# 32 of 256 prompt tokens go from the dense value products to gathered rows, and gate times activation is formed in place late in the score stage

## What is computed

```python
# per token: eid (8 heads x 16 picks), gate = softmax(top_s)
act = gelu(einsum('chkd,cd->chk', u_emb[eid], xc))
out = einsum('chk,chkd->cd', gate * act, v_emb[eid])
x   = x + gate2 * out
```

## Time and profile before

| what | us |
|---|---|
| median of 3 runs | 1236.54 (1234.68 to 1238.4) |
| span of the profiled execution | 1236.2 |
| score stage, about | 428 to 868 |
| value stage, about | 868 to 1228 |
| TensorE busy | 1200.4 |
| VectorE / GpSimd / ScalarE busy | 920.6 / 617.2 / 596.2 |

### The profile page before, as it was taken

One profiled execution on the slowest core, in us unless ns is written; L12 is line 12 of the kernel. 1 busy time (PEld: TensorE's weight loads), 2 busy tenths in 40 slices (PEclk: granted clock), 3 DMA queues, 4 the chain that ended last, 5 costly groups with the idle time before them and its releaser, 6 DMA issues.

```text
span 1236.2 us, 28223 instructions
## 1 busy us (share of the span) xinstructions
PE 1200.4 (97%) x8839; PEld 1114.8 (90%) x8839; DVE 920.6 (74%) x2251; ACT 596.2 (48%) x1021; POOL 617.2 (50%) x313
## 2 busy tenths in 40 slices
PE   5999999989999999999999999999999999999997
PEld 3888888879989999999999999999888888888886
DVE  3899967957647999779999997000667888888865
ACT  2342546666444445445555454444555555555553
POOL 0475665603755577766666666777203444443101
PEclk9999999999999999999999999999999999999999
DMA  9786674424643466665555555667877898888773
GB/s 356 247 294 211 221 254 176 159 69 164 243 149 125 138 216 199 211 193 182 178 187 179 181 184 180 216 208 241 278 240 271 314 341 307 305 300 308 270 238 105
DMA packets 115996, 273.12 MB, mean 221 GB/s; under 512 B 32033, under 2 KB 56321, under 8 KB 115553
## 3 DMA queue, kind: packets, MB, share of 16 engines
q1 hardware_dynamic: 107760, 248.96, 59.5%
q0 software_dynamic: 6448, 19.71, 4.5%
q10 hardware_dynamic: 1728, 3.68, 0.9%
HBM read 249.30 MB, written 23.00 MB: 220 GB/s over the span
## 4 chain that ended last, share of the span: by engine, by line
PE 90%; issue 2%; DVE 2%; DMA 2%; POOL 2%; ACT 1%; SPq 1%; DVEq 0%; POOLq 0%; ACTq 0%
PE ps L2305 19%; PE ps L2247 11%; PE ps L2254 11%; PE ps L2248 11%; PE ps L2308 10%; PE ps L1909 7%; PE ps L1925 7%; PE ps L1919 6%; PE ps L2283 2%; DMA ring<-in_stream 2%; POOL split L683 1%; PE ps L1941 1%; PE ps L2013 1%; PE ps L1863 1%; PE ps L2224 1%
## 5 line engine op out<-in xcount | busy, mean ns | idle before, releaser
L750 POOL TENSOR_TENSOR split<-ring,split 128x1024 fp32r<-128x1024 f32 x128 | 307.4, 2402 | 138.7 <-ACT split L1051 138.7
L1051 ACT ACTIVATE split<-ring 128x1024 fp32r<-128x1024 f32 x256 | 271.6, 1061 | 173.5 <-PE ps L2305 168.4
L683 POOL TENSOR_TENSOR split<-ring,split 128x1024 fp32r<-128x1024 f32 x77 | 187.9, 2442 | 210.7 <-ACT split L862 204.1
L2247 PE MATMUL ps<-h2r,split 128*128 128x288 f32 x1024 | 278.6, 297 | 0.7 <-ACT big L1077 0.5
L2248 PE MATMUL ps<-h2r,split 128*128 128x288 f32 x1024 | 278.8, 296 | 0.0
L2305 PE MATMUL ps<-h2r,split 128*128 128x512 f32 x1016 | 255.3, 392 | 0.0
L2305 PEld LDWEIGHTS ps<-h2r,split 128*128 128x128 f32 x1016 | 182.8, 189 | 32.7
L2247 PEld LDWEIGHTS ps<-h2r,split 128*128 128x128 f32 x1024 | 192.9, 188 | 1.2 <-ACT big L1077 0.8
L2248 PEld LDWEIGHTS ps<-h2r,split 128*128 128x128 f32 x1024 | 192.4, 188 | 0.0
L1758 DVE TENSOR_TENSOR split<-ring,split 128x1024 fp32r<-128x1024 f32 x128 | 156.0, 1219 | 1.8 <-PE ps L2254 1.8
L1107 ACT ACTIVATE act<-ps 128x288 f32<-128x288 f32 x124 | 51.2, 413 | 219.0 <-PE ps L2254 215.9
(11 more groups left out here) (301 smaller groups left out, 1624.4 us busy)
## 6 DMA issues: line engine op xcount, KB each, us to landing
ring<-in_stream SPq DMA_DIRECT2D x371, 512.0 KB, 3.5
act_dram<-act SPq DMA_DIRECT2D x128, 128.0 KB, 1.7
big<-in_stream SPq DMA_DIRECT2D x20, 512.0 KB, 7.7
parts<-act_dram SPq DMA_DIRECT2D x16, 512.0 KB, 4.7
big<-act_dram SPq DMA_DIRECT2D x16, 512.0 KB, 5.4
big<-in_cache_k SPq DMA_DIRECT2D x16, 128.0 KB, 2.5
big<-in_cache_v SPq DMA_DIRECT2D x16, 128.0 KB, 3.4
s_act_dram<-act SPq DMA_DIRECT2D x128, 16.0 KB, 1.5
```

What stands on the lines that cost most here:

```text
L683: nc.gpsimd.tensor_tensor(split[:, n % 2, 1], ring[:, POS[CUT[n]] % R, :], split[:, n % 2, 0].bitcast(f32), ALU.subtract).then_inc(lin_lo, 1)
L750: nc.gpsimd.tensor_tensor(split[:, (n + ODD) % 2, 1], ring[:, slot_of(n), :], split[:, (n + ODD) % 2, 0].bitcast(f32), ALU.subtract).then_ ...
L1051: nc.scalar.activation(split[:, (n + ODD) % 2, 0], ring[:, slot_of(n), :], ACT.Copy).then_inc(hi_ready, 1)
L2247: MM(out, u_hi[:, k], h_hi[:, k], start=(k == 0), stop=False)
```

## The change

The last 32 prompt tokens (TS of them) leave gate_mat and the value products and are handled as the samples are. TG = 64 tokens are gathered, TW = 224 stay dense. So:

- The value products have 2 x 224 = 448 and 224 columns; MIXED becomes 224 / 4 = 56 chunks, AFTER 40.
- Picks: VectorE makes index and gate tables for the 32 tokens as well, and SyncE copies them into place in four small DMAs at chunk 32. s_act_dram has 64 tokens a row, act_dram 224.
- GpSimd gathers 64 rows and 64 score columns. Rows have five buffers, not three; scores come in 16 parts of four. VectorE's add_row runs four or five times in 8 chunks, from chunk 8 to chunk 118, into two sums.
- Gate times activation: gate_mat is multiplied in place. SyncE reads groups of four chunks back in the last 40 chunks of the score stage (load_again, three in four chunks), the last two groups in the value stage; VectorE multiplies 120 chunks before the value stage's first low and eight within it.
- TensorE folds the second sum in eight small products (prompt_rows) into columns 224 to 256 of the value banks, behind the first of the last four chunks.

```diff
-MIXED = TP // 4
+
+TG = 2 * TS
+TW = T - TG
+MIXED = TW // 4
 BEFORE = 32
 SOFTMAX = 16
 TURN = BEFORE - R
 AFTER = NSUB - MIXED - BEFORE
 assert BEFORE % R == 0 and MIXED % R == 0 and AFTER % R == 0 and NSUB % R == 0
...
+EARLY = (BEFORE + MIXED) // R
+AGAIN = 3
+LEFT_OVER = NSUB // R - AGAIN * (AFTER // R)
+assert 0 < LEFT_OVER <= 2 and AGAIN * (AFTER // R) <= NSUB // R - 1
...
-        rows = [rows_a[:, 0], rows_a[:, 1], big[:, 18 * TP:18 * TP + D]]
-        NROW = len(rows)
-        s_sum = tail.take(D)
-        act_odd = tail.take(R, TP)
+        tail.at = NSUB * TW
+        NROW = 5
+        rows = tail.take(NROW, D)
+        s_sum = tail.take(2, D)
+        act_odd = tail.take(R, TW)
...
 
-            with sp.Fori(0, NSUB // R - 2) as g:
+            with sp.Fori(0, BEFORE // R) as g:
                 u_turn(g)
...
+            sp.wait_ge(s_picked, 6)
+            for part in range(4):
+                sp.dma_start(pick_at[part * TS:(part + 1) * TS, :, TS:TG], aside_u[P - TS:P, :, part * TS:(part + 1) * TS])\
+                    .then_inc(moved, 16)
+            with sp.Fori(BEFORE // R, EARLY) as g:
                 u_turn(g)
 
-            def v_turn(g, b):
-
-                sp.wait_ge(w_lo, g * R)
-                sp.dma_start(act_bs[b], act_dram[:, bass.ds(g * R + R, R), :]).then_inc(act_loaded[b], 16)
+            def load_again(j):
+
+                if j < 2:
+                    sp.wait_ge(gate_copied, 2 * MIXED)
+                else:
+                    sp.wait_ge(weighted, R * (j - 1))
+                for s in range(2):
+                    sp.wait_ge(act_stored[s], 32 * (R // 2) * (j + 1))
+                sp.dma_start(act_bs[j % 2], act_dram[:, j * R:(j + 1) * R, :]).then_inc(act_loaded[j % 2], 16)
+
+            for g in range(EARLY, NSUB // R):
+                for n in range(R):
+                    load_expert(g * R + n, n)
+                    sp.wait_ge(gelued, g * R + (n + 1))
+                    sp.dma_start(act_dram[:, g * R + n, :], act[:, n % 2, 0:TW]).then_inc(act_stored[n % 2], 16)
+                    sp.dma_start(s_act_rows[g * R + n], act[:, n % 2, TW:T]).then_inc(act_stored[n % 2], 16)
+                    if n:
+                        load_again((g - EARLY) * AGAIN + n - 1)
+
+            for n in range(R):
+                load_expert(NSUB + n, n)
+                if n < LEFT_OVER:
+                    load_again(NSUB // R - LEFT_OVER + n)
+
...
+            with sp.Fori(1, 11) as g:
+                v_turn(g)
...
+            sp.wait_ge(w_lo, 24)
             sp.dma_start(xe, x_dram).then_inc(x_loaded, 16)
...
             pool.wait_ge(gate_copied, 2 * MIXED)
-            nc.gpsimd.memset(s_sum, 0.0).then_inc(row_zero, 1)
-            pool.wait_ge(s_picked, 3)
-            for j in range(2):
+            nc.gpsimd.memset(s_sum, 0.0).then_inc(zeroed, 1)
+            pool.wait_ge(moved, 16 * 5)
+            for j in range(NROW):
                 gather_row(j)
             for s in range(2):
                 pool.wait_ge(act_stored[s], 32 * NSUB // 2)
-            for j in range(TS):
-                if j == 2:
-
-                    pool.wait_ge(weighted, 18 + D // TP)
-                if j >= NROW:
+            for part in range(TG // R):
+                if part:
+
+                    pool.wait_ge(s_weighted, part)
+                for j in range(part * R, (part + 1) * R):
+                    gather_score(j)
+                for j in range(max(NROW, part * R + 1), min(TG, part * R + R + 1)):
                     pool.wait_ge(row_summed, j - NROW + 1)
-                if j >= 2:
                     gather_row(j)
-                gather_score(j)
...
+            def high_weights(c, n, first=False):
+                eng.wait_ge(weighted, c + 1)
...
+                mine = gate_mat[:, c] if isinstance(c, int) else gate_mat[:, bass.ds(c, 1)].rearrange("p o t -> p (o t)")
+                nc.scalar.activation(dst, mine, ACT.Copy).then_inc(w_hi, 1)
...
+            part = slice(P - TS, P)
+            theirs = eq.rearrange("p n a -> p (n a)")[part, P:3 * P].rearrange("p (w n) -> p w n", w=2)
+            step(V.scalar_tensor_tensor(theirs[:, 0], tsel[part, NQ - 1, 0], float(NSUB), tsel[part, NQ - 1, 1], ALU.mult,
+                                        ALU.add))
...
-                V.tensor_copy(pick_at[:, w], s_expert[:, w]).then_inc(s_picked, 1)
+                V.tensor_copy(pick_at[:, w, 0:TS], s_expert[:, w]).then_inc(s_picked, 1)
+                V.tensor_copy(aside_u[part, w], theirs[:, w]).then_inc(s_picked, 1)
+            V.tensor_copy(aside[part, 2], tsel[part, NQ - 1, 2]).then_inc(s_picked, 1)
...
-            def weights(g2, b, n):
-                dve.wait_ge(act_loaded[b], g2 * 16 + 16)
-                V.tensor_tensor(act_bs[b][:, n], act_bs[b][:, n],
-                                gate_mat[:, bass.ds(g2 * (2 * R) + (b * R + n), 1)].rearrange("p o t -> p (o t)"),
-                                ALU.mult).then_inc(weighted, 1)
-
-            def low(c, b, n, first=False):
+            def weights(c):
+                j, n = divmod(c, R)
+                dve.wait_ge(act_loaded[j % 2], 16 * (j // 2 + 1))
+                V.tensor_tensor(gate_mat[:, c], gate_mat[:, c], act_bs[j % 2][:, n], ALU.mult).then_inc(weighted, 1)
...
+            for c in range(NSUB - R * LEFT_OVER):
+                weights(c)
...
+            def scale_picks(part):
+
+                cols = slice(part * R, (part + 1) * R)
+                dve.wait_ge(score_in, 16 * R * (part + 1))
+                V.tensor_tensor(pick_act[:, cols], pick_act[:, cols], pick_gate[:, cols], ALU.mult).then_inc(s_weighted, 1)
+
+            def add_row(j):
+                slot, total = j % NROW, s_sum[:, j // TS]
+                dve.wait_ge(row_in[slot], 16 * (j // NROW + 1))
+                dve.wait_ge(s_weighted, j // R + 1)
+                if j:
...
-                V.scalar_tensor_tensor(s_sum, rows[slot], pick_act[:, bass.ds(j, 1)], s_sum, ALU.mult, ALU.add)\
+                V.scalar_tensor_tensor(total, rows[:, slot], pick_act[:, j:j + 1], total, ALU.mult, ALU.add)\
...
+            SPARSE = {1: 4, 2: 5, 3: 5, 4: 4, 5: 5, 6: 5, 7: 4, 8: 5, 9: 5, 10: 4, 11: 5, 12: 5, 13: 4, 14: 4}
+            ADDS = {4: (0, 2, 4, 6), 5: (0, 2, 3, 5, 7)}
+            assert sum(SPARSE.values()) == TG
+
+            dve.wait_ge(zeroed, 8)
+            j = 0
+            for g in range(NSUB // (2 * R)):
                 for i in range(2 * R):
-                    b, n = divmod(i, R)
-                    c = g2 * (2 * R) + i
-                    if first and i == 0:
-                        weights(g2, 0, 0)
-                    low(c, b, n, first and i == 0)
-                    slot = adds.index(i) if sparse is not None and i in adds else None
-                    if slot is not None:
-                        scale_pick(sparse * NROW + slot, sparse, slot)
-                    if i + 1 < 2 * R:
-                        weights(g2, (i + 1) // R, (i + 1) % R)
-                    elif not last:
-                        weights(g2 + 1, 0, 0)
-                    value_low(c, n, *((u_done, NSUB) if first and i < 2 else (o_done, c - 1)))
-                    if slot is not None:
-                        add_row(sparse * NROW + slot, slot)
-
-            SPARSE, TURNS = 3, TS // NROW
-            v_turns(0, first=True)
-            with dve.Fori(1, SPARSE) as g2:
-                v_turns(g2)
-            dve.wait_ge(row_zero, 1)
-            v_turns(SPARSE, sparse=0)
-            with dve.Fori(SPARSE + 1, SPARSE + TURNS) as g2:
-                v_turns(g2, sparse=g2 - SPARSE)
-            v_turns(SPARSE + TURNS, sparse=TURNS, adds=ADDS[:TS % NROW])
-            with dve.Fori(SPARSE + TURNS + 1, NSUB // (2 * R) - 1) as g2:
-                v_turns(g2)
-            v_turns(NSUB // (2 * R) - 1, last=True)
+                    c = g * (2 * R) + i
+                    low(c, i % R, c == 0)
+                    value_low(c, i % R, *((u_done, NSUB) if c < 2 else (o_done, c - 1)))
+                    if c < R * LEFT_OVER:
+                        weights(NSUB - R * LEFT_OVER + c)
+                    if g in SPARSE and i in ADDS[SPARSE[g]]:
+                        if j % R == 0:
+                            scale_picks(j // R)
+                        add_row(j)
+                        j += 1
...
                 def high(k):
-                    return MM(ps[k][:, 0:2 * TP], v[0][:, k], w_both, start=first, stop=last)
+                    out = ps[k][:, :].rearrange("p (a t) -> p a t", a=2)[:, :, 0:TW]
+                    return MM(out, v[0][:, k], w, start=first, stop=last)
 
                 def lower(k):
-                    return MM(ps[k][:, 0:TP], v[1][:, k], w[:, 0], start=False, stop=False)
+                    return MM(ps[k][:, 0:TW], v[1][:, k], w[:, 0], start=False, stop=False)
...
+
+            def prompt_rows():
+
+                pe.wait_ge(row_summed, TG)
+                for k in range(KC):
```

(3 more changed lines are left out.)

124 lines of the change are left out of this document (50 added, 74 removed).

## The result

The changed kernel takes 1225.54 us (median of five runs, 1225.38 to 1232.97) where the kernel before takes 1234.68 in the same comparison: a ratio of 0.9935, 95% interval 0.9909 to 0.9961. It is faster, by about 8 us going by the ratio and 9 by the medians. The forecast was 18 us: the time lies inside its range of 1202 to 1236, and the gain is half of what was forecast.

The account below looks back on a forecast made before the run. TensorE's own matmuls were taken as the bound, longest the value stage's 512-column product. Against the 1236.2 us span: -36.6 - 3.9 + 1.8 + 8.4 + 4.6 + 6 + 1.4 = -18.3, or 1218 us, range 1202 to 1236.

Parts of the forecast that it names:

- the seam's term: Between score and value stage: TensorE waits for the 30th activation load, four products and low(0); loss 8.4 us, 7.6 to 10.
- late score stage: Last score chunks: VectorE's 120 products, slowed by GpSimd's split, hold up SyncE's loads and stores; loss 6 us, bounds 0 and 14.
- value chunks: Value stage: each chunk gains 0.286 us, and 339 GB/s of ring loads and rows is still enough, so rows cost nothing.
- second stop: Early value stage: low(1) queues behind a product waiting for load 30, issued only after value_low(0); loss 4.6 us, 4 to 6.
- the port: Late score stage: VectorE instructions with two SBUF inputs stand still while GpSimd works, leaving three products per chunk at best.
- The wide and narrow products: Value stage: 448 and 224 columns take 1.63 and 0.89 us for eight products, gaining 36.6 us over 128 chunks.
- The floor of 111 ns: Value stage: a product with 128 new weight columns takes at least 111 ns, so the narrow one gains 9 ns, not 13.3.
- The gates: Score stage: 56 chunks carry gate products where 64 did; gain 3.9 us.
- The fold for the prompt rows: Last value chunks: eight products of 32 columns run as 16 records of 111 ns on the path; loss 1.8 us.
- (a): Rival for the whole kernel: the waits are hidden and only TensorE's own terms are left, 1197.5 us; chance 0.08.
- (b): Rival in the value stage: GpSimd's gathers become the bound and pace TensorE, 1254 us or 1326; chance 0.14.
- (c): Rival in the value stage: the narrow product under 256 columns runs as two records, 222 ns, giving 1332 us; chance 0.06.

Follow-up runs that it names:

- e5: Changed kernel with VectorE making GpSimd's split from score chunk 92 on, products three chunks behind loads, and a key-mask constant altered by mistake: 1217.5 us.
- e1: Changed kernel with the first five row gathers on GpSimd held until VectorE has made its 121st product: 1220.6 us.
- e9: Changed kernel with the first five row gathers waiting for VectorE's 120th product and products 120 to 127 placed behind value chunks 4 to 11: 1217.2 us.
- e3: Changed kernel with the products of chunks 0 to 119 multiplying by a PSUM tile in place of the activations read again: 1216.4 us.
- e0: The changed kernel run again unaltered, as yardstick for the other runs: 1227.5 us over eight runs, ratio 0.9922 to the kernel before.
- first profile: Profiled execution of the unaltered changed kernel in the first measurement, the longest of its five runs: 1232.97 us, span 1231.1.
- e2: Changed kernel with the products of chunks 120 to 127 made behind value chunks 4 to 11 in place of 0 to 7: 1223.3 us.
- e4: Changed kernel with the value stage's narrow product cut from 224 to 160 columns: 1227.4 us, one run.
- e6: Changed kernel with only the first five row gathers made, the other 59 left out, and adds taking the old rows: 1227.6 us.
- e8: Changed kernel with VectorE's split from chunk 92, 108 products before the value stage, the rest later, first five row gathers six score chunks apart: 1200.98 us, ratio 0.9727.
- e7: Changed kernel with VectorE's split from chunk 92, 108 products before the value stage, later products and three loads moved into it, key-mask constant altered: 1206.3 us.

## Why the prediction was wrong

**The step that failed** is the landing time inside the seam's term. The prediction worked out the stop itself: 30 groups in front of low(0), the 30th load behind the last store, 4.7 us of landing. Then it wrote "to 10 (five row gathers of 512 KB go out in the same microseconds)", 1.6 us for a collision that it had seen coming. The seam is the sum of three parts, the issue of load 29 behind score 127, its landing, and 1.7 us for four products and low(0) (1.6 in the forecast, which then rounded 876.7 up to 877):

| profile | load 29 issued behind score 127, us | issue to VectorE's product, us | seam, us |
|---|---|---|---|
| forecast | 2.9 | 4.7 | 9.5 |
| e5, rows long gone | 2.6 | 4.1 | 8.5 |
| e1 and e9, rows wait | 3.7 and 3.3 | 5.2 and 5.9 | 10.7 and 10.9 |
| e3, rows there | 2.8 | 8.4 | 13.0 |
| e0, rows there | 3.3 | 9.0 | 14.0 |
| first profile, rows there | 3.3 | 12.8 | 17.8 |
| e2, e4, e6, rows there | 6.0 to 6.1 | 10.9 | 18.6 to 18.8 |

Without the rows the load lands in 4.1 to 5.9 us, about as forecast; with them in 8.4 to 12.8, so the collision costs 3.7 to 8.1 us over the 4.7, and it got 1.6. Five gathers of 512 KB are 2.6 MB, some 7 us of the whole DMA at the 341 to 402 GB/s that the windows of that moment show. That sum could have been made from the earlier trace rows, where 301 GB/s took 84% of it. In e2, e4 and e6 another 3 us come from the issue: the load waits for VectorE's products of group 27 in its buffer, a wait that the prediction had for the late score stage and not for the last load.

How much each part carries depends on the execution. In e0, whose profiled time is its median, the seam is 4.6 us over the forecast, the value chunks 2 to 123 are 4.4 over (310.27 us, 30.5 below the kernel before), the late score stage 3.3, and the second stop is 1.7 under it.

**The value chunks** are the same mistake in small. "339 GB/s, which I take as still enough" put the rows at nothing. They cost 1.9 to 3.6 us over chunks 8 to 123, through ring loads that land late, and all of it is gone in e6. Another 0.7 us is the price itself: a chunk gained 0.280 us, from 2.793 to 2.513, where 0.286 was forecast.

**The late score stage** was right in mechanism and within its bounds (0 to 14), with a value below what this profile shows: 6 for 9.9. Seven profiles with the same score stage show 4.2 to 10.1. What decides is the port, and e3 and e5 settle it from two sides: 920 ns a product with two SBUF inputs and GpSimd at work, 382 with one of them in PSUM, 386 with GpSimd idle, and the stretch is at 89.60 both times (in e5 the 4.7 us of score chunks 94 and 95 lie in front of it). The earlier trace rows had shown it on two instructions. The Trainium skill ("SBUF — State Buffer", SBUF: two separate sides) calls the pair that both engines share an exclusive lock, held for the whole instruction, which binds a VectorE instruction with two SBUF inputs against a GpSimd instruction that reads SBUF, as its split does; the trace agrees: the longest product takes 2.62 us, where one beside an idle GpSimd takes 0.39.

**Right, with their numbers.** The wide and narrow products: 1.63 and 0.88 us for eight, forecast 1.63 and 0.89. The floor of 111 ns from the earlier trace rows is 106 ns at 160 columns; at 224 the measured 110 ns don't tell it from the columns at 2.4 GHz and 13 to 17 ns (106 to 110). The gates: 3.9 for 3.9. The fold for the prompt rows: 0.9 for 0.9. The second stop with the clock: 5.9 for 5.4 in the first profile; e2 splits it into 2 to 4 and 2.3, where the prediction had 4.6 and 1.4. In e0 the two chunks lost only 3.7. As written, 5 to 5.7 us less the 1.4 that chunk 0 covers are 3.6 to 4.3, not 4 to 6; the prediction doesn't say what fills the gap, and product and low(1) behind the load, 0.4 us each, would.

**The rivals.** (a), nothing but TensorE's own terms, 1197.5, was no forecast for this kernel, but e8 comes near it at 1201 once most of the waits are taken out. (b) fell: the page after gives the two gather lines

```profile
L793 POOL DMA_INDIRECT pick_act<-s_act_dram,pick_at x64 | 85.7, 1339 | 70.1 <-DVE pick_act L1802 44.1
L788 POOL DMA_INDIRECT big<-in_stream,pick_at x64 | 89.8, 1404 | 55.2 <-DVE big L1811 44.4
```

so a pair costs 1.40 + 1.34 us and 0.3 for each issue, 3.3 in place of 4.0, and it is GpSimd that waits for VectorE's adds, 44 us in all. (c) fell with the 0.88 us of the narrow products.

**What no term stood for:** the last store. It lands 3.2 us after its issue (1227.95 to the span's end at 1231.1) where it took 5.3 before, and these 2.1 us cover part of the miss. That is luck: in e6, with the same store, it took 5.7.

**What stays open.** With the same five rows going out, load 29 takes 8.4 to 12.8 us to land, and in three profiles the queue issues it 3 us later than in the others. The order in which rows, ring loads and the scattered sample store meet in the DMA engines would have to be followed packet by packet, and no run here did so.

## What to carry to other kernels

When a transfer becomes the last thing on the path, its price is the landing time under what else is in flight at that moment, not a median from a quiet stretch: add up the bytes of everything that the same event releases, here five prefetches of 512 KB, issued from 873.8 us on, the first of which was needed at 917.7. Prefetches without a deadline belong behind the transfer with one, or spread out, but not merely somewhere else (e7). And an engine that seems idle may be slow to use: ask for each new VectorE instruction how many inputs lie in SBUF and what GpSimd does meanwhile; an operand in PSUM (e3, which leaves the real product out) or moving GpSimd's work to VectorE itself (e5) removed the loss of that stretch.

## What the runs showed of the hardware beyond that

- VectorE's product with one operand in PSUM ran in 382 ns beside a GpSimd that was busy 2.4 us of every 3.2, as fast as with GpSimd idle (386).
- In the one run of e4, a product of 160 columns with new weights is hardly shorter than one of 224 (106 and 110 ns), and the 448-column products around it took 1.69 us for eight in place of 1.63.
- GpSimd's row gather was expected at 2.35 us, the median of the earlier trace rows; in the changed kernel its median is 1.13 and its mean 1.40, although VectorE is busier (216.6 of 250 us from 910 on, 204.2 from 900 on before). Why it was slow before was not looked into.
- After the 17.54 us without work in e2, TensorE ran the first value chunk at a granted clock of 0.50, the level of 1.2 GHz, and took 2.3 us longer than a chunk at 1.00; in e7 and e8, which have no such stop, the clock was 1.00 from 866 to 880 us.
